# Two mixer outputs of a hybrid trunk reordered, and the recurrence's tail laid beside the second one

## The reference

```
# layer 0: a mixed half ya and a convolution half yb
u, v = gelu(z[:, :A]), layernorm(gelu(z[:, A:2A]))
ya = u * (ws @ v + bs)                       # per chunk of 128 tokens, 4 groups
glu = zb[:, :B] * sigmoid(zb[:, B:])
yb = silu(rmsnorm(dwconv31(glu)))            # 31 taps
x += gate * (concat(ya, yb) @ w_out[0])
# layer 1: recurrence yc (8 heads, both directions) and attention yd
y = y_fwd + y_bwd
yn = (y - mean(y)) * rsqrt(var(y) + eps) * ln_g + ln_b      # per head
yc = (yn + bonus) * g,   g = sigmoid(xg @ g1) @ g2
x += gate * (concat(yc, yd) @ w_out[1])
```

## Time and profile before

| | us |
|---|---|
| median of 3 runs (lowest, highest) | 1999.63 (1998.32, 2001.02) |
| the profiled execution's own time | 2000.47 |
| its span in the profile | 1998.6 |
| TensorE busy | 1884.6 |
| VectorE busy | 1061.9 |
| ScalarE busy | 768.8 |
| GpSimd busy | 598.1 |

### The profile page before, as it was taken

The page is one execution under the profiler, slowest core; times in us unless marked ns, Lnnn a source line. Parts: engine busy times, 40 slices in busy tenths (PEclk is TensorE's granted clock), DMA queues, the critical chain, the costliest instruction groups (busy, mean ns, idle before and its releaser), DMA issues.

```text
span 1998.6 us, 43869 instructions
## 1 busy us (share of the span) xinstructions
PE 1884.6 (94%) x18252; PEld 1730.5 (87%) x18252; DVE 1061.9 (53%) x1864; ACT 768.8 (38%) x1216; POOL 598.1 (30%) x327
## 2 busy tenths in 40 slices
PE   6899899999999998999998998989799999999996
PEld 3765699999999998878877887878699999999996
DVE  4497755442144547947566666666455443144423
ACT  4111335552155435237454232323144553145521
POOL 2300153444244445211111111111044444344442
PEclk8999899999999999899998999999899999999998
DMA  8666332222122221120110000000022222122221
GB/s 346 269 263 231 133 131 80 74 81 73 67 73 73 89 69 42 51 75 33 43 60 2 3 3 3 3 3 3 7 74 74 73 73 87 61 74 73 81 77 62
DMA packets 35344, 159.67 MB, mean 80 GB/s; under 512 B 3936, under 2 KB 4448, under 8 KB 28560
## 3 DMA queue, kind: packets, MB, share of 16 engines
q1 hardware_dynamic: 32832, 152.02, 20.9%
q10 hardware_dynamic: 1872, 3.61, 0.5%
q0 software_dynamic: 512, 2.13, 0.3%
HBM read 154.73 MB, written 3.01 MB: 79 GB/s over the span
## 4 chain that ended last, share of the span: by engine, by line
PE 83%; DVE 7%; ACT 3%; issue 3%; POOL 2%; DMA 2%; SPq 0%; DVEq 0%; PEldq 0%; POOLq 0%; ACTq 0%; PEld 0%
PE ps L220 18%; PE ps L222 18%; PE ps L221 18%; PE ps L1931 10%; PE ps L1970 2%; PE ps L706 2%; PE ps L696 2%; PE ps L1910 2%; PE ps L366 2%; DMA arena<-in_mod_w 2%; PE ps L1506 1%; PE ps L1227 1%; PE ps L1508 1%; PE ps L1507 1%; PE ps L2054 1%
## 5 line engine op out<-in xcount | busy, mean ns | idle before, releaser
L259 POOL TENSOR_TENSOR w_lo<-wslot,w_hi 128x1024 fp32r<-128x1024 f32 x130 | 319.7, 2460 | 690.5 <-ACT w_hi L254 690.5
L220 PE MATMUL ps<-xa_hi,w_hi 128*128 128x322 f32 (+1 forms) x1440 | 446.1, 310 | 0.0
L222 PE MATMUL ps<-xa_hi,w_lo 128*128 128x322 f32 (+1 forms) x1440 | 446.0, 310 | 0.0
L221 PE MATMUL ps<-xa_lo,w_hi 128*128 128x322 f32 (+1 forms) x1440 | 444.9, 309 | 0.0
L220 PEld LDWEIGHTS ps<-xa_hi,w_hi 128*128 128x128 f32 x1440 | 271.8, 189 | 0.2
L254 ACT ACTIVATE w_hi<-wslot 128x1024 fp32r<-128x1024 f32 x130 | 138.1, 1062 | 347.2 <-PE ps L222 289.8
L221 PEld LDWEIGHTS ps<-xa_lo,w_hi 128*128 128x128 f32 x1440 | 271.3, 188 | 0.2
L222 PEld LDWEIGHTS ps<-xa_hi,w_lo 128*128 128x128 f32 x1440 | 271.2, 188 | 0.0
L1931 PE MATMUL ps<-arena 64*64 64x64 f32 (+2 forms) x5760 | 243.3, 238 | 15.0 <-DVE arena L2238 12.6
L1931 PEld LDWEIGHTS ps<-arena 64*64 64x64 f32 x5760 | 214.5, 136 | 31.4 <-DVE arena L2238 16.7
L220 PE MATMUL ps<-hid_hi,d_hi 128*128 128x320 f32 x704 | 218.0, 310 | 3.9 <-POOL hid_lo L1106 3.9
(11 more groups left out here) (214 smaller groups left out, 3315.8 us busy)
## 6 DMA issues: line engine op xcount, KB each, us to landing
arena<-in_mod_w SPq DMA_DIRECT2D x48, 1024.0 KB, 7.1
wslot<-in_ffn_up SPq DMA_DIRECT2D x88, 512.0 KB, 3.5
wslot<-in_ffn_down SPq DMA_DIRECT2D x32, 704.0 KB, 4.0
wslot<-in_cd_w SPq DMA_DIRECT2D x22, 512.0 KB, 3.5
wslot<-in_w_out SPq DMA_DIRECT2D x16, 512.0 KB, 3.5
wslot<-in_ab_w SPq DMA_DIRECT2D x12, 512.0 KB, 8.1
x<-in_x_fm SPq DMA_DIRECT2D x2, 1280.0 KB, 7.3
out_y<-arena ACTq DMA_DIRECT2D x8, 320.0 KB, 2.4
```

Of the source, the lines that this page charges most:

```text
L220: nc.tensor.matmul(out, wh[:, m], hi[:, kk, t], start=(kk == 0), stop=False)
L221: nc.tensor.matmul(out, wh[:, m], lo[:, kk, t], start=False, stop=False)
L222: last = nc.tensor.matmul(out, wl[:, m], hi[:, kk, t], start=False, stop=(kk == k_all - 1))
L259: pool.tensor_tensor(wl[:, :], wslot[:, s, 0:tile_cols[base]], wh[:, :], ALU.subtract).then_inc(lo_ready, 1)
```

## The change

First mixer: the last 13 steps of the taps run without a break, before the reciprocal of the deviation; ScalarE takes the variance's root before the gelus of u. The sums of the squares move ahead of u tile 3. The four mixes then run one behind the other (banks 0, 4, 2, 4), and output tiles 0 and 1 take the convolution's four chunks first and the mixed half's after. Modulation tiles 40 and 41 come before, 42 and 43 after the convolution's chunks. VectorE scales the convolution's rows before it takes the mixes; the first low row is made after mix 2, the rest after mix 3. ScalarE makes tile 1's high part after the second convolution row.

Recurrence: the gate's sums go ahead of the last outputs and are emptied by ScalarE. The drain and meeting is gone. ScalarE makes the weight parts and seven high rows after the last unit, GpSimd tile 0's low part and seven low rows after the last round, and TensorE takes the second output's chunks in the order 4, 5, 6, 7, 0, 1, 2, 3 (the host turns the weight rows to match). The last pair's affine, bonus and gate are put together as (bonus + ln_b) * g and ln_g * y * g, made while the root is awaited; behind the reciprocal stand one multiplication and one addition. The last row's low row is VectorE's.

```diff
+        Y_ORDER = [*range(KA, KD), *range(KA)]
         def chunk_of_ycat(pe, layer):
             before = (KD - BY_POOL) * (layer + 1) + KD * layer
-            return lambda kk: pe.wait_ge(src_lo["dve"], before + kk + 1)
-        def source_hi(act, a, hi, ks):
-            for k in ks:
-                nc.scalar.activation(hi[:, k, :], a[:, k, :], ACT.Copy).then_inc(src_hi, 1)
+            return lambda kk: pe.wait_ge(src_lo["dve"], before + Y_ORDER.index(kk) + 1)
+        def chunk_of_y1(pe):
+            def chunk(kk):
+                if kk < KD - 1:
+                    pe.wait_ge(src_lo["pool"], 2 * BY_POOL + kk + 1)
+                else:
+                    pe.wait_ge(src_lo["dve"], 2 * (KD - BY_POOL) + KD + 1)
+            return chunk
...
             def mix(g):
-                pe.wait_ge(drained[g % 2], ab["out"] + 1)
-                if g >= 2:
-                    pe.wait_ge(mix_used, g - 1)
+                if g % 2 == 0:
+                    pe.wait_ge(drained[g // 2], ab["out"] + 1)
+                elif g == 1:
+                    pe.wait_ge(root_ready, 2)
+                else:
+                    pe.wait_ge(mix_used, 2)
...
+                if n == 2:
+                    pe.wait_ge(vtm_ready, NT)
+                    rms_pe(pe, KD, KA)
             pe.wait_ge(vmul_ready, NT)
-            pe.wait_ge(vtm_ready, NT)
-            mix(0)
-            mix(1)
-            rms_pe(pe, KD, KA)
+            for g in range(4):
+                mix(g)
             mod_columns_pe(pe, 9)
-            mix(2)
-            mix(3)
+            mod_pe(pe, 40, 41)
+            pe.wait_ge(mix_used, 1)
+            out_part(0, range(KA, KD), True)
             pe.wait_ge(mix_used, 3)
+            out_part(1, range(KA, KD), False)
+            mod_pe(pe, 42, 43)
+            pe.wait_ge(mix_used, 4)
             out_part(0, range(KA), True)
-            pe.wait_ge(mix_used, 4)
             out_part(1, range(KA), False)
-            mod_pe(pe, 40, 41, 42, 43)
-            out_part(0, range(KA, KD), True)
-            out_part(1, range(KA, KD), False)
...
-            return 2 * (g % 2)
+            return (0, 4, 2, 4)[g]
...
             squares_of_conv(0)
+            act.wait_ge(var_ready, 1)
+            nc.scalar.activation(lnmv[:, :, 1], lnmv[:, :, 1], ACT.Sqrt, bias=eps_c[:, 0:1]).then_inc(std_ready, 1)
+            warm(act, ACT.Gelu_apprx_tanh)
             gelu_of_u(0)
             mod_act(act, 8)
             gelu_of_u(1)
-            act.wait_ge(var_ready, 1)
-            nc.scalar.activation(lnmv[:, :, 1], lnmv[:, :, 1], ACT.Sqrt, bias=eps_c[:, 0:1]).then_inc(std_ready, 1)
+            squares_of_conv(1)
+            gelu_of_u(2)
+            root_act(act, 1, KA, 0)
+            tile_hi(act, ab["out"], 0, 0)
             warm(act, ACT.Gelu_apprx_tanh)
-            gelu_of_u(2)
             gelu_of_u(3)
             mod_act(act, 9)
-            for s in range(2):
-                tile_hi(act, ab["out"], 0, s)
-            squares_of_conv(1)
-            root_act(act, 1, KA, 0)
             warm(act, ACT.Silu)
             for k in range(KA):
-                act.wait_ge(ya_ready, k + 1)
-                nc.scalar.activation(y_hi[:, k, :], ycat[:, k, :], ACT.Copy).then_inc(src_hi, 1)
-            for k in range(KA):
+                if k == 2:
+                    tile_hi(act, ab["out"], 0, 1)
                 act.wait_ge(yn_ready, k + 1)
                 nc.scalar.activation(ycat[:, KA + k, :], ycat[:, KA + k, :], ACT.Silu,
                                      scale=pcol("b_norm", k)).then_inc(yb_ready, 1)
                 act.wait_ge(yb_ready, k + 1)
                 nc.scalar.activation(y_hi[:, KA + k, :], ycat[:, KA + k, :], ACT.Copy).then_inc(src_hi, 1)
+            for k in range(KA):
+                act.wait_ge(ya_ready, k + 1)
+                nc.scalar.activation(y_hi[:, k, :], ycat[:, k, :], ACT.Copy).then_inc(src_hi, 1)
...
-            taps(4, {2: 18, 3: 18})
+            taps(13, {2: 18, 3: 18})
+            st.wait()
+            dve.sem_inc(conv_ready, 1)
...
-            taps(9, {2: 22, 3: 22})
-            st.wait()
-            dve.sem_inc(conv_ready, 1)
+            rms_dve(dve, st, 1)
+            for k in range(KA):
+                for a, b, v in GROUPS:
+                    last = nc.vector.tensor_tensor(ycat[:, KA + k, a:b], conv[:, k, a + PAD * v:b + PAD * v], rs[:, a:b], ALU.mult)
+                last.then_inc(yn_ready, 1)
             dve.wait_ge(bs_ready, 1)
+            def y_lo_of(k):
+                if k >= KA:
+                    dve.wait_ge(mix_ready, 4)
+                else:
+                    dve.wait_ge(ya_ready, KA)
+                dve.wait_ge(src_hi, KD + Y_ORDER.index(k) + 1)
+                nc.vector.tensor_tensor(y_lo[:, k, :], ycat[:, k, :], y_hi[:, k, :], ALU.subtract).then_inc(src_lo["dve"], 1)
...
+                if g == 2:
+                    y_lo_of(KA)
+            for k in Y_ORDER[1:]:
+                y_lo_of(k)
             mod_dve(dve, st, 9)
-            for k in range(KA):
-                dve.wait_ge(ya_ready, k + 1)
-            source_lo(dve, "dve", KD, ycat, y_hi, y_lo, range(KA))
-            rms_dve(dve, st, 1)
-            for k in range(KA):
-                for a, b, v in GROUPS:
-                    last = nc.vector.tensor_tensor(ycat[:, KA + k, a:b], conv[:, k, a + PAD * v:b + PAD * v], rs[:, a:b], ALU.mult)
-                last.then_inc(yn_ready, 1)
-            source_lo(dve, "dve", KD, ycat, y_hi, y_lo, range(KA, KD))
...
-            todo += [(END, [("mean", "dve", 2), ("var", "act", 2), ("gate", "dve", 2)])]
+            todo += [(END, [("gate", "act", 2), ("mean", "dve", 2), ("var", "act", 2)])]
...
                 chain(LAST, r)
+            for g in range(2):
+                round_of((END, "gate", g), scan_w[:, HP - 1, 2 * P:3 * P], lg)
             outputs(LAST)
...
+            wait(emptied["act"], entry[END, "var", 1][2])
+            wait(emptied["dve"], entry[END, "mean", 1][2])
...
+            wait(emptied["dve"], entry[LAST, "RM", 2][2])
+            tile_hi(act, cd["out"], 0, 0)
+            tile_hi(act, cd["out"], 0, 1)
+            for n in range(KD - 1):
+                nc.scalar.activation(y1_hi[:, n, :], ycat1[:, Y1_OF[n], :], ACT.Copy).then_inc(src_hi, 1)
+            for g in range(2):
+                take_bank((END, "gate", g), half(last_gate, g), half_bank((END, "gate", g)))
             tail_square(END, HP - 1)
             tail_root(END)
+            act.wait_ge(last_y, 1)
+            nc.scalar.activation(y1_hi[:, KD - 1, :], ycat1[:, Y1_OF[KD - 1], :], ACT.Copy).then_inc(src_hi, 1)
+        Y1_OF = (4, 5, 6, 7, 0, 1, 2, 3)
...
+            y, bonus = ycat1[:, HP - 1, :], rkv[:, KA + HP - 1, :]
+            wait(emptied["act"], entry[END, "gate", 1][2])
+            wait(emptied["dve"], entry[LAST, "bonus", 1][2])
+            wait(emptied["dve"], entry[END, "mean", 1][2])
+            st(nc.vector.scalar_tensor_tensor(out=bonus, in0=bonus, scalar=pcol("ln_b", HP - 1), in1=last_gate, op0=ALU.add, op1=ALU.mult))
+            st.wait()
+            st(nc.vector.scalar_tensor_tensor(out=last_gate, in0=y, scalar=pcol("ln_g", HP - 1), in1=last_gate, op0=ALU.mult, op1=ALU.mult))
             for part in range(4):
                 tail_root(END, part)
-            tail_norm(END, HP - 1)
-            tail_affine(HP - 1)
-            tail_add(HP - 1)
-            tail_gate(END, HP - 1)
+            st.wait()
+            wait(tail_sq, HP)
+            st(nc.vector.tensor_tensor(y, last_gate, rs[:, :], ALU.mult))
+            st.wait()
+            nc.vector.tensor_tensor(y, y, bonus, ALU.add).then_inc(last_y, 1)
...
+            tile_lo(pool, cd["out"], 0, 0)
+            for n in range(KD - 1):
+                pool.wait_ge(src_hi, 3 * KD + n + 1)
+                pool.tensor_tensor(y1_lo[:, n, :], ycat1[:, Y1_OF[n], :], y1_hi[:, n, :], ALU.subtract).then_inc(src_lo["pool"], 1)
             pool.wait_ge(fin_out, 16)
+            pool.wait_ge(last_y, 1)
+            tile_lo(pool, cd["out"], 0, 1)
...
-            pass_gate(dve, 1)
-            source_lo(dve, "dve", 3 * KD, ycat1, y1_hi, y1_lo, range(KD))
+            dve.wait_ge(src_hi, 4 * KD)
+            nc.vector.tensor_tensor(y1_lo[:, KD - 1, :], ycat1[:, Y1_OF[KD - 1], :], y1_hi[:, KD - 1, :],
+                                    ALU.subtract).then_inc(src_lo["dve"], 1)
```

More of the change, by code:

```diff
@@ L210, in build, with product_of_parts @@
         BY_HALF = ((0, HALF), (HALF, T))
-        def product_of_parts(base, s, ks, k_all, hi, lo, halves=BY_HALF):
+        def product_of_parts(base, s, ks, k_all, hi, lo, halves=BY_HALF, first=0, end=None):
             wh, wl = tile_parts(base, s)
@@ L219, in product_of_parts @@
                     out = ps[:, 2 * s + h, 0:b - a]
-                    nc.tensor.matmul(out, wh[:, m], hi[:, kk, t], start=(kk == 0), stop=False)
+                    nc.tensor.matmul(out, wh[:, m], hi[:, kk, t], start=(kk == first), stop=False)
```

(24 more changed lines are left out.)

11 lines of the change are left out of this document (5 added, 6 removed).

## The result

The changed kernel takes 1992.42 us (1991.61 to 1993.74) against 1999.93 before, six runs of each: ratio 0.9965, 95% interval 0.9954 to 0.9975. It is faster, by 7.5 us, about half of the 14.3 forecast and just inside the range. The profiled execution took 1992.44, with 1990.6 of span.

The account below looks back on a forecast made before the run. TensorE, busy 94% of the span, was taken to bound the kernel. First mixer 5.4 plus tail 8.9 made 14.3 off 2000.47, so 1986.2; less 0.8 to the median, 1985.3, said as 1985; range 1979 to 1992.5.

Parts of the forecast that it names:

- part 2: Recurrence's tail and second mixer's output: product 0 ends at 1452.8 against 1461.7, gain 8.9, bounds 5 to 11.
- Gate sums and outputs: Tail, TensorE: gate sums put ahead make the last outputs 1.5 late, done at 1433.9; y added by 1434.8.
- Mean: Tail: the mean sums end at 1437.4 and the mean is ready at 1438.0.
- Early chunks: Second output, TensorE: seven chunks start at 1441.9, 18 matmuls at 0.27, the rest at 0.15, done about 1450.3.
- Reciprocals: Tail, VectorE: run from 1442.7 to 1446.9; in the gain's lower bound of 5 each waits in part beside GpSimd.
- Last low row: Tail: collides with GpSimd's tile 1 low part started at 1448.8, takes 2.46, ready at 1451.9.
- Product 0: Second output's first product: the last chunk adds 0.9 to 1451.9, ending at 1452.8 against 1461.7.
- Part 1: First mixer's output: tile 2 at 245.5 instead of 252.1, 6.6 less 1.2 for the clock: 5.4, bounds 2.5 to 8.5.
- half effect: Rival: only one part delivers (conv sums late, or modulation tile 43 late), 6 to 9 gained, 1992; chance 0.12.
- serial tail: Rival: GpSimd and VectorE exclude each other completely, tail grows by up to 10.4, 1995.7; chance 0.07.
- low clock: Rival: TensorE stays at 1.2 GHz through both outputs, 192 matmuls at 0.12 more each, 7.5 slower, 2007; chance 0.05.
- the prediction's own test: Both outputs: a last low row later than 1454, or tile 2 later than 249, would make the forecast wrong.

Follow-up runs that it names:

- each part alone: Only the first mixer's edits against the kernel before: 1995.54 us, ratio 0.9981; only the recurrence tail's edits: 1994.24 us, ratio 0.9975.
- the tail alone: Only the recurrence tail's edits, with the old first mixer, against the kernel before: 1994.24 us, ratio 0.9975.
- a fifth: Changed kernel with GpSimd making both weight tiles' low parts early, its state transfer still ahead of the seven rows: 1987.08 us, ratio 0.9932 to the kernel before.

## Where the prediction failed, and where it held

**The failed step** stands in part 2: VectorE "does bonus and affine by the gate (0.82 each, both with two SBUF inputs): each may wait one GpSimd row, so 1442.7". The first was passed over at four row ends and got in at the fifth, 7.83. The rule of one row was the right price where GpSimd had issued no transfer just ahead: 1.78 and 2.05 with the rows early, 0.92 and 2.04 with the transfer last or on SyncE. Missing was that GpSimd's own transfer ahead of the run turns the waiting of one row into waiting for them all. I had costed that transfer only as a wait "over by then". With the transfer last and nothing else changed, product 1 ended 10.1 earlier than before, counted from the end of the rounds, and not 3.4: the step cost 6.7 us, more than the whole shortfall of the tail.

That kernel took 1985.01, just what the forecast says, but this is partly luck: by position the tail then gained 10.1 for 8.9, the first mixer 3.9 for 5.4, and 2.7 came from the stages in between, which the forecast had left at nothing.

The tail's terms, 4.9 us added to put them on the clock of before:

- Gate sums and outputs: forecast done at 1433.9, measured 1429.0 + 4.9 = 1433.9. The added y 1434.8, measured 1434.7. Right to 0.1, by two errors that cancel: the gate sums made the outputs 2.0 late and not 1.5, and the outputs took 1.75 for 2.21.
- Mean: 1438.0, measured 1436.7. The mean sums ran at full clock (1.34) and not at half (2.51).
- Early chunks: forecast from 1441.9 to 1450.3 with 18 matmuls at half clock, measured from 1439.5 to 1445.9 with all 42 at full clock. So TensorE then stood idle for 8.7, where the forecast had 1.6.
- Reciprocals: forecast to start at 1442.7, measured 1445.5. This is the fold: 2.8 late in spite of the 1.3 before it, so 4.1 against the forecast's own price.
- Reciprocals beside GpSimd: in the changed kernel they came after its run (4.18). Beside it, in three experiments, they took 4.17 to 4.19. The bound in which each waits in part is gone.
- Last low row: 1451.9, measured 1454.5; its collision was forecast at 2.46 and took 2.36.
- Product 0: 0.9 behind the row, measured 2.1, and tile 1 took 8.90 (1451.70 to 1460.60) where the kernel with extra matmuls took 7.04. I gave the last chunks no clock price, with the idle stretch forecast short: 1.2 + 1.9.

8.9 less 2.6 (row), 1.2 and 1.9 (clock) is 3.2; measured 3.4.

**Part 1** went as laid out: sums before u tile 3, no wait for tile 43, waits of 2.24 and 1.30 for 2.2 and 1.7. The first low part was there at 228.86 - 1.48 = 227.4 on the clock of before, for 227.5, but by two errors that cancel: the multiply took 3.01, over my bound of 2.46, and from its start at 223.55 my own terms, 2.3 and 0.8, give 226.65 and not 227.5. In the sum one size was off: "I take 1.2 of 0 to 2.4" for the clock; it was 2.6. The excess of 1.4 is nearly the whole of 5.4 - 3.9 = 1.5. The prediction's evidence for a middle value was a stretch of small matmuls, which does not answer for 320-column passes.

**Rivals.** The half effect ("only one part delivers", 1992) named the right time for the wrong reason: each part alone gains 4 to 5. The serial tail had the right mechanism, VectorE and GpSimd excluding each other, but not through the whole tail: its price was up to 10.4, and what was lost to the shut-out was 6.7. The low clock ruled nineteen and some 23 matmuls, not 192. In the prediction's own test, "tile 2 later than 249" came true at 249.66 only with the 1.48 of the late start, and the last low row "later than 1454" did come true on the clock of before (1454.5).

The Trainium skill (SBUF — State Buffer, "SBUF: two separate sides") gives the pair shared by VectorE and GpSimd to whichever starts first, for the whole instruction, where VectorE's has two SBUF inputs. The 3.01 of the multiply that started 0.05 after GpSimd's part agrees, and so do the 0.88 of the folds that read PSUM; the earlier trace rows, where VectorE's recorded start was 0.04 the earlier, does not. What decided here was who gets the pair when GpSimd's next instruction and a waiting VectorE one both want it: turns (2.04), or GpSimd every time (7.82).

**Open.** What ends the shut-out. In the changed kernel the fold was still passed over 12.0 us after the issue (1437.53 against 1425.55) of a transfer that lands within 2.3 us by the record of its queue. With GpSimd's pause of 2.37 it was gone, but there the next two-input instruction came to a row's end only 14.4 us after the issue, so the pause and the mere time can't be told apart. No run had the transfer ahead of the rows with a pause right behind it. Why GpSimd's issuing does it was not tried either, nor was the cause of the 2.5 between 780 and 1000.

## What to carry to other kernels

Where VectorE has two-SBUF-input work beside GpSimd, look at what GpSimd issued last: keep its DMAs behind its run, or give them to another engine, and let the operand that can stay in PSUM stay there. An idle stretch of TensorE cost its length plus 2.6 or 2.7 us of lower clock here, where dense 320-column work followed, and spare matmuls in the wait bought that back in the stretch itself; whether the kernel's time keeps it has to be measured. When an early stretch of work is moved beside a chain, first ask whether it could end before the chain starts. When the gains of the parts seem to add up to the time, look also at the stages in between: here 2.5 us lay there, and their cause is open.

## What the runs showed of the hardware

- A VectorE instruction with two SBUF inputs beside back-to-back GpSimd subtractions waited for the end of the row it met, 2.05 us at most beside these rows of 1.5. With a DMA issued by GpSimd just ahead of the run it waited to the run's end: 7.8 in four kernels (the changed one, the tail alone, each of the two with extra matmuls in the changed kernel) and 5.44 in a fifth.
- These instructions with one SBUF input were not delayed: reciprocals 4.17 to 4.19 for four beside the rows and 4.18 without them, folds from PSUM 0.88, the add from PSUM 0.82. A copy with one SBUF input was: 2.39 for 0.16 beside GpSimd's subtraction at 805.19.
- A GpSimd subtraction of 2.4 took 7.43 where a VectorE instruction of 5.49 with two SBUF inputs had started 0.26 before it.
- Turns cost GpSimd too: seven rows 10.60 undisturbed, 11.09 with one VectorE instruction let in, 11.79 with two.
- Two waits of 2.24 and 1.30 a microsecond apart cost as much clock (2.6, granted 0.50) as one of 8.7 (2.7, granted 0.51). After a wait of 1.14 it stayed at 1.00.
